# The rotated halves of retention's queries and keys: two VectorE products across partition halves in place of a TensorE product with a sign matrix

## The chip, the cores and the metric

One Trainium2 chip, one NeuronCore of it. The metric is the device time of the whole program in microseconds (us), the median of several executions. TensorE (PE), VectorE (DVE), ScalarE (ACT), GpSimd (POOL) and SyncE (SP, which here only issues DMA) each run a program of their own and meet only at semaphores.

## The reference

Two blocks of two layers each are run one after the other on 512 positions of width 1024, all in float32. The change lies in the first block. Each of its two layers has three branches (a gated MLP, a retention branch, a gated delta rule). What matters here is the retention branch, four heads of width 128:

```python
def rotary(x):
    ...
    x1, x2 = x[..., : hd // 2], x[..., hd // 2:]
    return jnp.concatenate([x1 * cos - x2 * sin, x2 * cos + x1 * sin], axis=-1)

def retention_branch(q, k, v, z, decay_logit, norm_g):
    q = rotary(q)
    k = rotary(k) * (RET_HD ** -0.5)
    ...                      # scores = q k^T times a decay mask, then times v, over all 512 positions
```

So each of the 8 tiles (4 heads of q, 4 of k) needs x * cos plus the tile with its two halves swapped, one of them negated, times sin.

## The kernel before

Activations are held feature-major: a tile is 128 features (partitions) by 512 positions. Weights come in granules of 512 KB that SP loads into four buffers `raw`; ACT rounds each to `wh` (`hi`, L1688), POOL computes the rest `wl = raw - wh` in two instructions of 128x512 (L2288), and PE multiplies with both parts of both operands, so one output tile is 8 x 3 matrix products of 128x512 (`feature_tile`, L827 to L829). A granule's buffer is reused four granules later; ACT rounds the next one right after it has copied the finished tile out of PSUM.

Granules 12 to 19 of each layer are the four query tiles and the four key tiles of retention. For each, in order of i = 0 to 7:

- PE runs `feature_tile(12 + i)`. After i = 0 it adds a few small products (`decay_sums`), after i = 1 the 16 products of `token_mix` for the gated MLP. From i = 1 on it then runs `rotate(i - 1)`, one float32 product of the sign matrix `rot` with tile i - 1, and after the last tile also `rotate(7)`. `rotate` writes one of PSUM banks 4 to 7 (bank 7 and 6 are called `pair` in the rows). It waits for ACT's copy of the tile, and for the bank to be free (`y_ready` for the first four, `rot_taken` for the others).
- ACT copies the finished tile to `qraw[i % 4]` (L1748; from i = 4 on it waits for `rot_taken` of tile i - 4), then rounds the granule g + 4.
- DVE first finishes `token_mix` (L2609, L2610), prepares two decay masks (`mask_arg`, L2617 to L2619), and then for each tile forms `rt2` = rotated x sin (L2626), `rt1` = qraw x cos (L2627) and their sum (L2630), into `rqT` for queries and into a part of `y` for keys.

Then PE runs `scores(0)` (L983, four products), and for each head `scores(h + 1)` and the products with the values (L994). DVE multiplies each score tile by its mask (`pb`, L2637) and frees its bank; `scores(1)` waits for the first `pb` of head 0. DVE executes in program order, so it comes to the first `pb` only when all eight tiles are rotated. Twelve more feature tiles (20 to 31) follow, with retention's normalisation and turns (`retention_turns`, L1004) between the first of them.

The DVE program has its own semaphore on which `step` and `inc` wait after each instruction. DVE_OWN counts such steps.

Of the kernel before, what the change touches and what calls it, by code (L numbers as in the profile page):

```python
# [18 lines left out]
ALU = mybir.AluOpType  # L19
# [3 lines left out]
P = 128  # L23
# [16 lines left out]
SUB = 1 << BASE  # L40
# [9 lines left out]

CON = {}
_at = 0
for _name, _n in (("ident", 128), ("ones", 128), ("rot", 128), ("cos", 512), ("sin", 512), ("dist", 896),
                  ("tri", 256), ("neg", 256), ("level", 2 * LEVELS * 128), ("own", 4), ("turn", 4)):
    CON[_name] = slice(_at, _at + _n)
    _at += _n
# [3 lines left out]
def constants():  # L60

    c = np.zeros((P, N_CON), np.float32)
    i = np.arange(P)
    c[:, CON["ident"]] = np.eye(P)
    c[:, CON["ones"]] = 1.0
    rot = np.zeros((P, P), np.float32)
    rot[i[:64] + 64, i[:64]] = -1.0
    rot[i[:64], i[:64] + 64] = 1.0
    c[:, CON["rot"]] = rot
    inv = (np.float32(10000.0) ** (-np.arange(0, P, 2, dtype=np.float32) / np.float32(P))).astype(np.float32)  # L70
    ang = (np.arange(T, dtype=np.float32)[None, :] * inv[:, None]).astype(np.float32)
    c[:, CON["cos"]] = np.tile(np.cos(ang), (2, 1))
    c[:, CON["sin"]] = np.tile(np.sin(ang), (2, 1))
    c[:, CON["dist"]] = np.arange(896)[None, :] - i[:, None] - 384
    before = (i[:, None] <= i[None, :]).astype(np.float32)
    c[:, CON["tri"]] = np.concatenate([before, before.T], 1)
    c[:, CON["neg"]] = (np.concatenate([before, before.T], 1) - 1.0) * np.float32(1e30)
    level = np.zeros((P, 2, LEVELS, P), np.float32)
    for s in range(LEVELS):
        b = SUB << s  # L80
        same = (i[:, None] // (2 * b)) == (i[None, :] // (2 * b))
        m = same & ((i[:, None] // b) % 2 == 0) & ((i[None, :] // b) % 2 == 1)
        level[:, 0, s] = m
        level[:, 1, s] = m.T
    c[:, CON["level"]] = level.reshape(P, -1)
    c[:, CON["own"]] = (i[:, None] // SUB) == np.arange(4)[None, :]
    forward = (i % SUB) < SUB // 2
    c[:, CON["turn"]] = np.stack([np.where(forward, 1.0, -1.0), forward, ~forward, 0.0 * i], 1)
    return c
# [39 lines left out]
def layer_signals(nc):  # L129
    per = dict(  # L130
        x_ready=8, sq_ready=8, sq_added=6, norm_sd=1, norm_rec=1, ht_ready=8, hh_ready=8, hl_ready=8,
        proj_taken=44, wab_hi=1, wab_lo=1, ab_rows=1, ab_done=3, beta_ready=1, log_args=2, log_done=2,
        g_ready=1, egc_ready=1, nbeg_ready=1, norm_spread=2, l2_spread=8,
        vhat_sd=4, vhat_ready=4, lnvar=4, mix_done=4, y_ready=8, y_gated=8,
        rot_done=8, rot_taken=8, rope_ready=8,
        arg_ready=4, mask_ready=4, score_done=16, p_ready=16, o_done=4, o_taken=4,
        gn_var=1, gn_sd=1, gn_ready=4, gn_turned=4,
        conv_ready=12, silu_ready=12, nsq_ready=8, l2_done=8, l2_sd=8, l2_rec=8, l2_ready=8,
        kt_done=4, ktok_ready=4, vt_done=4, vtok_ready=4,
        blocks_done=1, blocks_out=2, arg_small=1, exp_small=1, solved=2, gz_ready=4, gz_taken=4,  # L140
        rows_done=8, kq_done=4, ag_ready=8, e_ready=16, lt_ready=8, st_ready=8, ub_ready=8,
        last_ready=8, qg_ready=8, lm_ready=16, y0_ready=8, x0_ready=8,
        p1_done=16, p1_ready=16, a_done=16, inv_ready=24,
        rhs_ready=24, wt_done=8, wt_ready=8,
        vn_done=32, vn_ready=32, s_done=24, s_ready=24, out_done=32, go_sq=4, go_ss=8, go_sd=4, go_rec=4, yc_raw=4,
        z_mul=4,
        yh_ready=12, yl_ready=12, gate_taken=24, merged=24, mh_ready=8, ml_ready=8, xl_ready=8,
        dve_own=DVE_OWN, act_own=ACT_OWN,
    )
    return {k: Signal(nc, k, v) for k, v in per.items()}  # L150

DVE_OWN = 126 + 2 * (SUB - 1)
ACT_OWN = 3


# [299 lines left out]
def build(nc, stream, params, consts, consts2, gains, xin, memin, out, n_granules):  # L457
    cur = [16512]

    def sb(name, shape, dt=F32, at=None):  # L460
        size = -(-int(np.prod(shape[1:])) * 4 // 32) * 32
        if at is None:
            at = cur[0]
            cur[0] += size
        assert at + size <= 229344, name
        return nc.alloc_sbuf_tensor_at(name, shape, dt, offset=at)
# [35 lines left out]
    C = {k: con[:, v] for k, v in CON.items()}  # L502
# [5 lines left out]
    ident, ones = C["ident"], C["ones"]  # L508
# [20 lines left out]
    qraw = [sb(f"qraw{i}", [P, T]) for i in range(4)]  # L529
    mask = [sb(f"mask{i}", [P, 896]) for i in range(2)]  # L530
    mtmp = sb("mtmp", [P, 896])
    rt2 = sb("rt2", [P, T])
# [78 lines left out]
    spare = sb("spare", [P, 1])  # L611
# [3 lines left out]
    for i in range(2):  # L615
        def tiles_at(n, count, at, shape=(P, T), dt=F32):
            return [sb(f"{n}_{i}_{t}", list(shape), dt, at=at + t * int(np.prod(shape[1:])) * 4) for t in range(count)]
        b = BUF[i]
# [51 lines left out]
    bk = [b[:, :] for b in bank] + [pair[:, 0:T], pair[:, T:2 * T]]  # L670
# [66 lines left out]
    with block:  # L737
# [85 lines left out]
        def _(pe):  # L823
            mm = nc.tensor.matmul
# [23 lines left out]
            with pe.Fori(0, DEPTH) as L:  # L848
                G = L * G_LAYER

                def wait(sig, n):
                    pe.wait_ge(s[sig].sem, s[sig].at(L, n))

                def inc(ins, sig):
                    ins.then_inc(s[sig].sem, 1)
# [20 lines left out]
                def feature_tile(g):  # L876

                    weights(g)
                    taken(g)
                    w = g % SLOTS  # L880
                    for k in range(KD):
                        m = three(bk[g % 4], wh[w][:, k * P:(k + 1) * P], wl[w][:, k * P:(k + 1) * P],
                                  hh[:, k], hl[:, k], k == 0, k == KD - 1)
                    m.then_inc(granule_done, 1)
# [53 lines left out]
                def decay_sums():  # L938

                    wait("g_ready", 1)  # L940
                    wait("beta_ready", 1)
                    for d in range(2):
                        m = mm(bk[6][:, 64 + d * 16:80 + d * 16], tri[d], gdec[:, :, d, :], start=True, stop=True)
                    inc(m, "ab_done")
# [10 lines left out]

                def rotate(i):
                    wait("proj_taken", 13 + i)
                    if i < 4:  # L960
                        wait("y_ready", i + 1)
                    else:
                        wait("rot_taken", i - 3)
                    inc(mm(bk[4 + i % 4], C["rot"], qraw[i % 4][:, :], start=True, stop=True), "rot_done")

                for i in range(8):
                    feature_tile(12 + i)
                    if i == 0:
                        decay_sums()
                    if i == 1:  # L970
                        token_mix()
                    if i:
                        rotate(i - 1)
                rotate(7)

                def scores(h):
                    wait("rope_ready", 5 + h)
                    for b in range(NT):
                        if h:
                            wait("p_ready", 4 * h + b - 3)  # L980
                        else:
                            wait("rot_taken", 5 + b)
                        inc(mm(bk[4 + b], rkT[h][:, b * P:(b + 1) * P], rqT[h][:, :], start=True, stop=True),  # L983
                            "score_done")

                scores(0)
                for h in range(H):
# [3 lines left out]
                    for b in range(NT):  # L991
                        wait("p_ready", 4 * h + b + 1)
                        for c in range(NT):
                            m = mm(bk[h][:, c * P:(c + 1) * P], pb[h % 2][b][:, c * P:(c + 1) * P], rv[b][:, h * P:(h + 1) * P],  # L994
                                   start=(b == 0 and c == 0), stop=(b == NT - 1), skip_group_check=True)
# [68 lines left out]
                for h in range(H):  # L1064
# [62 lines left out]
                    for st in range(NT):  # L1127
                        for d in range(2):
                            c = st if d == 0 else NT - 1 - st
# [13 lines left out]
                        for d in range(2):  # L1143
                            c = st if d == 0 else NT - 1 - st
# [1366 lines left out]
        def _(dve):  # L2511
            V = nc.vector
# [27 lines left out]
            with dve.Fori(0, DEPTH) as L:  # L2540
                step = Steps(dve, s["dve_own"], L)

                def wait(sig, n):
                    dve.wait_ge(s[sig].sem, s[sig].at(L, n))
# [3 lines left out]
                def inc(ins, sig):  # L2548

                    ins.then_inc(s[sig].sem, 1)  # L2550
                    count[sig] += 1
                    wait(sig, count[sig])
# [69 lines left out]
                mask_arg(1)  # L2622

                for i in range(8):
                    wait("rot_done", i + 1)
                    step(V.tensor_tensor(rt2[:, :], bk[4 + i % 4], C["sin"], ALU.mult))  # L2626
                    inc(V.tensor_tensor(rt1[:, :], qraw[i % 4][:, :], C["cos"], ALU.mult), "rot_taken")  # L2627
                    wait("rot_taken", i + 1)
                    dst = rqT[i][:, :] if i < 4 else rkT[i - 4]
                    inc(V.tensor_tensor(dst, rt1[:, :], rt2[:, :], ALU.add), "rope_ready")  # L2630
# [116 lines left out]
                for h in range(H):  # L2747
# [37 lines left out]
                    for st in range(NT - 1):  # L2785
                        for d in range(2):
                            c = st if d == 0 else NT - 1 - st
# [15 lines left out]
                with dve.Fori(0, 3) as n:  # L2803
                    B = L * 3 + n
                    G = L * G_LAYER
                    wait("dve_own", DVE_OWN)
                    for q in range(2):
# [552 lines left out]
```

## Time and profile before

| | |
|---|---|
| median of 3 runs | 2737.86 us (2737.37 to 2738.4) |
| profiled execution, first to last instruction | 2738.6 us |
| TensorE busy | 2660.0 us, 97% |
| VectorE busy | 1084.0 us, 40% |
| ScalarE busy | 1139.7 us, 42% |
| GpSimd busy | 1384.8 us, 51% |

The profile gives one execution's span, no other time of it; that span is 0.7 us above the median of the runs. The first layer's tiles 12 to 19 and its scores lie at about 94 to 180 us, the second layer's 677.4 us later. Matrix products are pipelined, so a row of 0.39 us does not mean that the next one starts 0.39 us later.

### The profile page before, as it was taken

What the parts mean: (1) busy time and instruction counts of PE and PEld (TensorE: products, weight loads), DVE (VectorE), ACT (ScalarE), POOL (GpSimd) and SP (SyncE); (2) the same over time, 40 slices, a digit from 0 to 9 for tenths busy, and PEclk for the clock granted to TensorE, in tenths of its full rate; (3) what the DMA queues carried; (4) which work ended last, traced back from release to release, by engine and by line L of the source; (5) the groups of instructions that cost most, each with busy time, mean ns of one, the idle gap of its engine ahead of it and who ended that gap; (6) DMA issues with size and microseconds to landing.
All of it is one profiled execution on the core that took longest, in us unless ns stands there. A gap on an engine that the chain in (4) does not pass through costs nothing.

```text
span 2738.6 us, 37589 instructions
## 1 busy us (share of the span) xinstructions
PE 2660.0 (97%) x13032; PEld 2158.2 (79%) x13032; DVE 1084.0 (40%) x2191; ACT 1139.7 (42%) x1732; POOL 1384.8 (51%) x1056
## 2 busy tenths in 40 slices
PE   7999999999999999999999999999999989999999
PEld 6768898888876889888887647888887755888887
DVE  3576643113466664312366563211104375221100
ACT  5437444324542744432455643333315464333321
POOL 5424665556642466655674213556547502466553
PEclk9999999999999999999999999999999999999999
DMA  5212111233221211123332112232333301233322
GB/s 179 83 44 75 41 32 40 99 99 125 86 85 39 70 40 31 47 93 99 123 103 75 32 31 70 93 100 92 100 113 109 92 8 40 78 108 98 100 93 76
DMA packets 62351, 215.10 MB, mean 79 GB/s; under 512 B 7296, under 2 KB 10496, under 8 KB 61824
## 3 DMA queue, kind: packets, MB, share of 16 engines
q1 hardware_dynamic: 62208, 213.28, 24.3%
q8 instruction: 79, 1.29, 0.2%
q14 instruction: 64, 0.52, 0.1%
HBM read 211.16 MB, written 2.10 MB: 78 GB/s over the span
## 4 chain that ended last, share of the span: by engine, by line
PE 82%; DVE 9%; issue 4%; POOL 2%; ACT 1%; DMA 0%; POOLq 0%; DVEq 0%; SPq 0%; ACTq 0%
PE bank L827 21%; PE bank L829 21%; PE bank L828 21%; PE pair L827 2%; PE pair L829 2%; PE pair L828 2%; PE pair L1530 2%; PE bank L994 1%; PE bank L1489 1%; PE bank L1490 1%; PE bank L1512 1%; DVE pair L2712 1%; DVE prod L2711 1%; POOL EG L2366 1%; PE pair L1343 1%
## 5 line engine op out<-in xcount | busy, mean ns | idle before, releaser
L2288 POOL TENSOR_TENSOR wl<-raw,wh 128x512 fp32r<-128x512 f32 x768 | 1036.3, 1373 | 1175.5 <-ACT wh L1919 380.8
L827 PE MATMUL bank<-hh,wh 128*128 128x512 f32 x1536 | 607.4, 395 | 3.7 <-DVE y L2799 2.3
L829 PE MATMUL bank<-hh,wl 128*128 128x512 f32 x1536 | 599.0, 390 | 0.0
L828 PE MATMUL bank<-hl,wh 128*128 128x512 f32 x1536 | 598.9, 390 | 0.0
L827 PEld LDWEIGHTS bank<-hh,wh 128*128 128x128 f32 x1536 | 289.1, 188 | 66.5 <-issue 5.6
L828 PEld LDWEIGHTS bank<-hl,wh 128*128 128x128 f32 x1536 | 289.1, 188 | 61.7 <-issue 2.9
L829 PEld LDWEIGHTS bank<-hh,wl 128*128 128x128 f32 x1536 | 288.9, 188 | 60.9
L2239 ACT CAST wh<-raw 128x1024 fp32r<-128x1024 f32 x120 | 125.5, 1048 | 254.0 <-PE pair L829 140.2
L827 PE MATMUL bank<-wh,hh 128*128 128x512 f32 (+2 forms) x352 | 140.6, 399 | 13.8 <-POOL wl L2288 12.4
L1919 ACT CAST wh<-raw 128x1024 fp32r<-128x1024 f32 x84 | 86.9, 1048 | 128.0 <-PE bank L829 108.5
L829 PE MATMUL bank<-wh,hl 128*128 128x512 f32 (+2 forms) x352 | 135.1, 384 | 0.0
L828 PE MATMUL bank<-wl,hh 128*128 128x512 f32 (+2 forms) x352 | 135.0, 384 | 0.0
L2812 DVE TENSOR_TENSOR gs<-gs,bank 128x512 f32<-128x512 f32 x24 | 16.4, 684 | 286.3 <-PE bank L829 286.3
L1688 ACT CAST wh<-raw 128x1024 fp32r<-128x1024 f32 x104 | 108.9, 1049 | 42.9 <-DMA raw<-stream 18.8
L1872 ACT CAST wh<-raw 128x1024 fp32r<-128x1024 f32 x72 | 75.3, 1046 | 85.5 <-PE pair L829 43.8
L3186 DVE TENSOR_TENSOR at<-row,bank 128x512 f32<-128x512 f32 x44 | 30.3, 689 | 202.2 <-PE bank L829 199.4
L827 PE MATMUL bank<-ah,wh 128*128 (+1 forms) x264 | 102.7, 389 | 0.0
L828 PE MATMUL bank<-al,wh 128*128 (+1 forms) x264 | 102.7, 389 | 0.0
L829 PE MATMUL bank<-ah,wl 128*128 (+1 forms) x264 | 102.7, 389 | 0.0
L1888 ACT ACTIVATE gs<-bank 128x512 f32<-128x512 f32 x48 | 28.8, 599 | 166.6 <-PE bank L829 166.5
L3183 DVE TENSOR_TENSOR at<-row,bank 128x512 f32<-128x512 f32 x44 | 30.3, 688 | 162.7 <-PE bank L829 162.1
L827 PEld LDWEIGHTS bank<-wh,hh 128*128 128x128 f32 x352 | 67.7, 192 | 26.1 <-issue 14.6
(465 smaller groups left out, 5235.8 us busy)
## 6 DMA issues: line engine op xcount, KB each, us to landing
raw<-stream SPq DMA_DIRECT2D x384, 512.0 KB, 3.5
mraw<-memin SPq DMA_DIRECT2D x3, 1024.0 KB, 5.5
par<-params SPq DMA_DIRECT2D x2, 1124.5 KB, 9.3
out<-xT SPq DMA_DIRECT2D x8, 256.0 KB, 2.0
con<-consts SPq DMA_DIRECT2D x1, 1540.0 KB, 15.7
xT<-xin SPq DMA_DIRECT2D x1, 1536.0 KB, 8.6
xT<-xin SPq DMA_DIRECT2D x1, 512.0 KB, 3.8
con<-consts SPq DMA_DIRECT2D x1, 512.0 KB, 3.2
```

Of the source, the lines that this page charges most:

```text
L827: mm(o, ah, bh, start=start, stop=False)
L828: mm(o, ah, bl, start=False, stop=False)
L829: return mm(o, al, bh, start=False, stop=stop)
L1530: x = mm(bk[value_bank(i, phase, a)], vv, pts[a % 2][kb][:, :], start=(kb == 0), stop=(kb == nk - 1))
L1688: nc.scalar.copy(wh[g % SLOTS][:, :], raw[g % SLOTS][:, :]).then_inc(hi_ready, 1)
L1872: nc.scalar.copy(wh[g % SLOTS][:, :], raw[g % SLOTS][:, :]).then_inc(hi_ready, 1)
L1888: A(gs[e][:, :], bk[e], ACT.Sigmoid).then_inc(s["gate_taken"].sem, 1)
L1919: nc.scalar.copy(wh[g % SLOTS][:, :], raw[g % SLOTS][:, :]).then_inc(hi_ready, 1)
L2239: nc.scalar.copy(wh[slot][:, :], raw[slot][:, :]).then_inc(hi_ready, 1)
L2288: m = TT(wl[slot][:, c], raw[slot][:, c], wh[slot][:, c].bitcast(F32), ALU.subtract)
L3183: V.tensor_tensor(at_[j][:, :], row[:, :], bk[2 * j], ALU.mult).then_inc(t["f_gate"].sem, 1)
L3186: V.tensor_tensor(at_[j][:, :], row[:, :], bk[2 * j + 1], ALU.mult).then_inc(t["f_up"].sem, 1)
```

## The change

The sign matrix goes from the constants (its 128 columns stay as unused space, so that no other column moves). `rotate` and its eight calls go from PE, with the signal `rot_done`. On DVE each tile's `rt2` now comes from `qraw` in two products of 64 partitions by 512: output partitions 0 to 63 from input partitions 64 to 127, and the other way round, with a sine table whose upper 64 rows carry the minus sign. Between these two and the product with the cosine there is no wait, where the `step` after L2626 was one. DVE waits for ACT's copy (`proj_taken`) instead of PE's product. `scores(0)` no longer waits for `rot_taken`.

```diff
-for _name, _n in (("ident", 128), ("ones", 128), ("rot", 128), ...
+for _name, _n in (("ident", 128), ("ones", 128), ("spare", 128), ...
...
-    rot = np.zeros((P, P), np.float32)
-    rot[i[:64] + 64, i[:64]] = -1.0
-    rot[i[:64], i[:64] + 64] = 1.0
-    c[:, CON["rot"]] = rot
...
-    c[:, CON["sin"]] = np.tile(np.sin(ang), (2, 1))
+    c[:, CON["sin"]] = np.concatenate([np.sin(ang), -np.sin(ang)])
...
-DVE_OWN = 126 + 2 * (SUB - 1)
+DVE_OWN = 118 + 2 * (SUB - 1)
...
-                def rotate(i):
-                    wait("proj_taken", 13 + i)
-                    if i < 4:
-                        wait("y_ready", i + 1)
-                    else:
-                        wait("rot_taken", i - 3)
-                    inc(mm(bk[4 + i % 4], C["rot"], qraw[i % 4][:, :], start=True, stop=True), "rot_done")
-
                 for i in range(8):
                     feature_tile(12 + i)
                     if i == 0:
                         decay_sums()
                     if i == 1:
                         token_mix()
-                    if i:
-                        rotate(i - 1)
-                rotate(7)
 
                 def scores(h):
                     wait("rope_ready", 5 + h)
                     for b in range(NT):
                         if h:
                             wait("p_ready", 4 * h + b - 3)
-                        else:
-                            wait("rot_taken", 5 + b)
...
                 for i in range(8):
-                    wait("rot_done", i + 1)
-                    step(V.tensor_tensor(rt2[:, :], bk[4 + i % 4], C["sin"], ALU.mult))
+                    wait("proj_taken", 13 + i)
+                    for low in (0, P // 2):
+                        to, of = slice(low, low + P // 2), slice(P // 2 - low, P - low)
+                        V.tensor_tensor(rt2[to, :], qraw[i % 4][of, :], C["sin"][of, :], ALU.mult)
                     inc(V.tensor_tensor(rt1[:, :], qraw[i % 4][:, :], C["cos"], ALU.mult), "rot_taken")
```

## Rows read from the trace of the kernel before

**Rows 1.** The page: busy time, and the chain that ended last.

```profile
PE 2660.0 (97%) x13032; PEld 2158.2 (79%) x13032; DVE 1084.0 (40%) x2191; ACT 1139.7 (42%) x1732; POOL 1384.8 (51%) x1056
...
PE 82%; DVE 9%; issue 4%; POOL 2%; ACT 1%; DMA 0%; POOLq 0%; DVEq 0%; SPq 0%; ACTq 0%
```

**Rows 2.** Chain in order of time, first layer (start us, us, what).

```profile
116.75 0.86 PE bank L964 x2
...
155.14 0.70 DVE pb L2637
155.88 1.98 PE bank L983 x4
```

**Rows 3.** Timeline of DVE, first layer.

```profile
119.05 2.06 DVE L2619 TENSOR_TENSOR mask<-mask,mtmp 128x896 f32<-128x896 f32 x1
...
143.10 0.69 DVE L2626 TENSOR_TENSOR rt<-bank,con 128x512 f32<-128x512 f32 x1 [3.23 <-PE bank L964]
143.82 0.69 DVE L2627 TENSOR_TENSOR rt<-qraw,con 128x512 f32<-128x512 f32 x1
144.62 1.60 DVE L2630 TENSOR_TENSOR y<-rt,rt 128x512 f32<-128x512 f32 x1
...
152.57 0.69 DVE L2626 TENSOR_TENSOR rt<-pair,con 128x512 f32<-128x512 f32 x1
153.30 0.91 DVE L2627 TENSOR_TENSOR rt<-qraw,con 128x512 f32<-128x512 f32 x1
154.31 0.69 DVE L2630 TENSOR_TENSOR y<-rt,rt 128x512 f32<-128x512 f32 x1
```

**Rows 4.** Timeline of POOL, first layer.

```profile
102.39 2.54 POOL L2288 TENSOR_TENSOR wl<-raw,wh 128x512 fp32r<-128x512 f32 x2 [2.13 <-ACT wh L1688]
...
118.54 3.72 POOL L2288 TENSOR_TENSOR wl<-raw,wh 128x512 fp32r<-128x512 f32 x2 [7.40 <-ACT wh L1688]
...
143.93 3.44 POOL L2288 TENSOR_TENSOR wl<-raw,wh 128x512 fp32r<-128x512 f32 x2 [2.91 <-ACT wh L1688]
150.27 3.39 POOL L2288 TENSOR_TENSOR wl<-raw,wh 128x512 fp32r<-128x512 f32 x2 [2.90 <-ACT wh L1688]
```

**Rows 5.** Timeline of ACT, first layer.

```profile
148.52 0.60 ACT L1748 ACTIVATE qraw<-bank 128x512 f32<-128x512 f32 x1 [3.81 <-PE bank L829]
```

**Rows 6.** Timeline of PE: first rotation, scores of head 1, products with the values.

```profile
110.16 1.10 PE L964 MATMUL bank<-qraw,con 128*128 128x512 f32 x2 [0.18 <-DVE y L2610]
...
159.42 3.73 PE L994 MATMUL bank<-rv,pb 128*128 128x128 f32 x32
...
833.31 3.57 PE L983 MATMUL bank<-rqT,y 128*128 128x512 f32 x4 [0.49 <-DVE pb L2637]
...
838.54 3.73 PE L994 MATMUL bank<-rv,pb 128*128 128x128 f32 x32
```

**Rows 7.** Stretches (PE busy and granted clock, PEclk): both layers, the waits for DVE.

```profile
198.69:202.10 3.41, 1.92 (x14) 1.27 (x13) 3.05 (x5) 2.59 (x4) 0.96 (x1) 1.00 0.03 13
...
830.17:833.57 3.40, 1.51 (x4) 0.56 (x4) 3.01 (x5) 0.00 (x0) 0.92 (x1) 1.00 0.42 118
833.57:836.98 3.41, 3.41 (x5) 1.34 (x5) 3.02 (x5) 0.00 (x0) 0.00 (x0) 0.50 0.09 36
...
878.00:881.35 3.35, 1.87 (x15) 1.27 (x13) 2.99 (x5) 2.71 (x4) 1.08 (x1) 1.00 0.06 22
881.40:888.10 6.70, 6.70 (x20) 5.44 (x20) 4.32 (x5) 1.59 (x3) 1.55 (x2) 0.50 0.26 78
```

**Rows 8.** Timeline of PE at the kernel's start.

```profile
12.44 0.79 PE L827 MATMUL bank<-wh,hh 128*128 128x512 f32 x1 [12.44 <-POOL wl L2288]
...
17.73 0.42 PE L827 MATMUL bank<-wh,hh 128*128 128x512 f32 x1
```

**Rows 9.** Timeline of DVE between the layers: neighbours with no wait between them.

```profile
684.46 0.67 DVE L2821 TENSOR_TENSOR xT<-xT,bank 128x512 f32<-128x512 f32 x1
685.06 0.74 DVE L2526 SCALAR_TENSOR_TENSOR hl<-xT,par,hh 128x512 fp32r<-128x512 f32 x1
```

More of the change, by code:

```diff
@@ L52 @@
 _at = 0
-for _name, _n in (("ident", 128), ("ones", 128), ("rot", 128), ("cos", 512), ("sin", 512), ("dist", 896),
+for _name, _n in (("ident", 128), ("ones", 128), ("spare", 128), ("cos", 512), ("sin", 512), ("dist", 896),
                   ("tri", 256), ("neg", 256), ("level", 2 * LEVELS * 128), ("own", 4), ("turn", 4)):
@@ L134, in layer_signals @@
         vhat_sd=4, vhat_ready=4, lnvar=4, mix_done=4, y_ready=8, y_gated=8,
-        rot_done=8, rot_taken=8, rope_ready=8,
+        rot_taken=8, rope_ready=8,
         arg_ready=4, mask_ready=4, score_done=16, p_ready=16, o_done=4, o_taken=4,
```

## The prediction

> **What bounds the kernel now.** I read the page first: PE is busy 97% of the span and holds 82% of the chain that ended last, DVE 9% [rows 1]. That says where time usually goes, not what this change meets, so I read the chain of waits through the stage of the change next. There PE passes from feature tile to feature tile, and each rotation stands in its path with 0.86 us (two passes of a float32 product) [rows 2]. At the stage's end the chain leaves PE: the last rotations and the first `pb` are DVE's, 155.14, and PE's scores of head 1 follow at 155.88 [rows 2]. So two clocks matter: PE's through the eight tiles, DVE's at the end. The timelines of DVE, POOL and ACT show how close they are.
>
> **What the change takes from PE.** Eight products per layer. Up to the end of tile 19 six of them lie on its path: the first costs its 0.86 plus 0.18 of waiting for `y` [rows 6], 1.0; five more 0.86 each [rows 2]. Together 5.3 us: ACT's copy of tile 19 starts at 143.2 instead of 148.52 [rows 5]. The last two rotations go from behind it. If nothing else held the stage, the first `pb` could come one rotation after that copy: 143.8 plus 3.0 (below), some 146.8, which is 8.3 us earlier than 155.14, in each layer.
>
> **What it gives to DVE.** Before, a tile cost product from PSUM, product with cosine, sum: starts at 143.82 and 144.62 give 0.80 from the second to the third; 152.57 and 153.30 give 0.73 from first to second; the sum takes 0.69 plus 0.03 [rows 3]. That is 2.25 us. After, there is one product more. No row shows a 64-partition operation. The nearest rows are products of the same 512 columns at 0.69 [rows 3]; bounds are 0.35 if half the partitions cost half, and 1.38 if a crossing costs double. I take 0.69, since nothing in the rows ties time to anything but columns. For the spacing of neighbours with no wait between them the rows give 0.60 (684.46 to 685.06) [rows 9], with a wait 0.73; I take 0.73, the nearer row, since it is the same kind of product in the same place. So 2.98 us per tile, 23.8 for eight. With the shorter spacing for the two freed gaps the eight tiles would take 8 x 2 x 0.13, some 2 us, less. The Trainium skill, "VectorE: DVE Perf Modes", section "Two Vector instructions with no wait between them", speaks for this choice: an instruction whose input or output starts in another group of 32 partitions than the last one's is held until the earlier ones are finished. By it the sum stays, without it the 2 us go; no row here shows a held pair.
>
> **What it takes away: PSUM was outside POOL's way.** The sum at 144.62 takes 1.60 instead of 0.69, and the cosine product at 153.30 takes 0.91; both read two SBUF operands while POOL works on `wl` [rows 3, 4]. The PSUM product at 152.57 keeps its 0.69 in the midst of POOL's pair 150.27 to 153.66. And POOL's pair grows from 2.54 undisturbed to 3.44 [rows 4]. The ends fit a strict alternation: POOL's first operation starts when the cosine product ends at 144.51, holds some 1.0 us, the sum runs 145.53 to 146.22, POOL's second ends at 147.37. So one POOL operation costs a waiting DVE product up to 1.0 us. Before, DVE idled between tiles and met POOL mostly once per tile. After, all four operations of a tile read SBUF, and DVE hardly idles.
>
> **The schedule of DVE, first layer.** It comes free for the rotations at 119.05 + 2.06 = 121.1 [rows 3]. POOL's pair for the tile that ends before was asked for at 118.54 [rows 4]; it comes 1.0 earlier (the first rotation is gone), falls before the last two mask operations instead of between them, and both its parts now delay them: DVE is free at 122.1. POOL's pair comes 1.75 us after a copy (150.27 behind 148.52) [rows 4, 5] and pairs are 6.34 apart (143.93 to 150.27), 5.5 without the rotation between. So the five further pairs are asked for at 145.0 for tile 19 and at about 139.5, 134.0, 128.5 and 123.0 before it. Ten operations, each holding DVE 0.95 (gaps take the rest), are 9.5. 122.1 + 23.8 + 9.5 = 155.4 for the end of the last sum; before it was 154.31 + 0.69 = 155.0 [rows 3]. DVE never waits for a copy on the way: the last at 143.8 is there long before the eighth tile's turn at 152.4. So the first `pb` comes 0.4 us later than before, less 0.1 for the freed waits: I take 0.3 per layer, 0.6 in all. The 8.3 us saved on PE turn into PE's wait for the first `pb`. `scores(0)` is done by 148 (it needs only the fifth rotation, at about 144.5, then 3.4 us), and behind it on PE's queue everything waits until about 156.2: 8 us. From there on both kernels run alike.
>
> **The clock.** That wait is longer than any in the middle of this kernel. In the second layer PE is busy 1.51 of 3.40 us, then the granted clock is 0.50, the lower of the two levels (1.2 GHz), for 3.41 us, and 1.00 after [rows 7]. Its price can be read: the products with the values start at 159.42 and 838.54, 679.12 apart, where the layers lie 677.43 apart (155.88 to 833.31, the scores just before): 1.7 us [rows 2, 6]. At the start of the kernel, after idleness, PE stays at the lower level from 12.44 until 17.7, 5.3 us [rows 8], worth 2.6; the fall at 881.40 lasts 6.70, worth up to 3.3 [rows 7]. The scores behind the new wait are bound by PE, so the price is paid. First layer, where there was no fall: bounds 1.7 and 3.3, I take 2.4. Second layer, which paid 1.7: bounds 0 and 1.6 more, I take 0.8. Sum 3.2.
>
> **Sum.** Rotations on DVE +0.6, clock +3.2: +3.8. Against the profiled span of 2738.6 this is 2742.4; that span stands 0.7 above the median, so 2741.7 for the median. One thing more may move with it, and I put it in the range only: at 878.00 PE is busy 1.87 of 3.35 and the clock falls for 6.70 us, while in the first layer 1.92 of 3.41 at 198.69 lead to no fall (1.00 there) [rows 7]. So close a decision can turn over when the stage arrives 3 us later, in either layer: plus or minus 3.3.
>
> **Rivals.** A measurement of this kernel can tell about 0.2%, 5.5 us, from no change.
>
> (a) DVE becomes the bound and gives all of PE's time back, the clock adds a little: +3.8, likeliest, 0.55. Its own range is 0 to +10, 2738 to 2748.
>
> (b) DVE keeps up. For it speaks that DVE idles 3.23 us before the sixth tile (143.10) [rows 3]. If the half products cost 0.35 each, the same schedule ends near 149.5, 5.6 earlier per layer; PE's idleness is then some 2 us, a fall as dear as the one there was: -11 +2, about 2729. If POOL did not stop it at all, near 146.9, 8.2 earlier per layer: 2721. Against it: rows tie cost to columns, and the stops are plain. Chance 0.13, 2721 to 2732.
>
> (c) DVE is slower than I count, and ends on the other side: a product that crosses partition halves costs more than one that does not. Sixteen of them per layer, with DVE the bound: each 0.1 us more is 3.2 us over both layers. From 0.12 more on the time is over the bound; at 1.38 each it would be +22, 2764. For it: no row shows one. Against it: nothing does so either. Chance 0.15, typically 2745 to 2765.
>
> (d) The neighbours with no wait overlap as in [rows 9]: 2 us less per layer, the wait shorter, one fall instead of more: about 2737. Chance 0.17. That the change does not take the rotations off PE at all is no case: the calls are gone.
>
> **How the numbers follow.** Slower by over 0.2% (above 2743.3): from (a) 0.17, where the clock turns over or falls twice, and (c) 0.12: 0.29. Faster (below 2732.4): (b) 0.12 and 0.01 of (d): 0.13. Within: 0.58. The range leaves out most of (b) and the far half of (c): 2732 to 2749.
>
> **What would show it.** Tile 19's copy near 143.2; sixteen half products per layer at 0.69 where POOL is still and up to 1.7 where it is not; no idle time of DVE between 122 and 155; PE without work from 148 to 156 with DVE named as releaser; first `pb` at 155.4; the granted clock at 0.50 behind it in both layers. A first `pb` before 152 would make the prediction wrong, and show that POOL's stops or the half products were counted too dear; one after 157 the reverse.

## The result, and the profile after

The kernel after takes 2746.78 us (median of 12 runs, 2744.95 to 2748.7), the kernel before 2738.86 (12 runs of the same sessions, 2736.18 to 2742.34). The ratio is 1.0026, 95% interval 1.0018 to 1.0035: 7.9 us slower by the medians. The likeliest case of the forecast said 3.8 slower, 2741.7; the range, 2732 to 2749, holds the time, which lies just past the 0.2% that the prediction called "slower" (it gave that a chance of 0.29; the interval begins at 0.18%). The profiled execution after has a span of 2744.2, against 2738.6 before. In every run on record the span is 1.8 us shorter than the run's time, so the execution profiled before stands for some 2740.4 us, 1.5 above its median, and the one after (2745.97) lies 0.8 below its own: the two profiles differ by 5.6 us, the medians by 7.9.

The page of the kernel after: busy time, then the chain that ended last, by engine ([rows 1] are before). PE is busy 7.9 us less, yet the span is longer: PE's idle time grew from 78.6 to 92.1 us, and of the work taken away (some 14 us, below) nearly half came back as a slower clock.

```profile
PE 2652.1 (97%) x13000; PEld 2156.0 (79%) x13000; DVE 1103.9 (40%) x2207; ACT 1140.0 (42%) x1732; POOL 1383.2 (50%) x1056
...
PE 80%; DVE 11%; issue 4%; POOL 2%; ACT 1%; DMA 0%; DVEq 0%; POOLq 0%; SPq 0%; ACTq 0%
```

The timeline of DVE after, first layer, against [rows 3]. Each tile is four operations now: two half products (L2611), the cosine product (L2612) and the sum (L2615).

```profile
120.90 1.09 DVE L2602 TENSOR_TENSOR mask<-mask,mtmp 128x896 f32<-128x896 f32 x1
122.11 2.40 DVE L2611 TENSOR_TENSOR rt<-qraw,con 64x512 f32<-64x512 f32 x2
124.53 1.69 DVE L2612 TENSOR_TENSOR rt<-qraw,con 128x512 f32<-128x512 f32 x1
126.31 0.69 DVE L2615 TENSOR_TENSOR rqT<-rt,rt 128x512 f32<-128x512 f32 x1
127.13 1.39 DVE L2611 TENSOR_TENSOR rt<-qraw,con 64x512 f32<-64x512 f32 x2
128.53 1.69 DVE L2612 TENSOR_TENSOR rt<-qraw,con 128x512 f32<-128x512 f32 x1
130.32 1.59 DVE L2615 TENSOR_TENSOR rqT<-rt,rt 128x512 f32<-128x512 f32 x1
...
152.73 1.39 DVE L2611 TENSOR_TENSOR rt<-qraw,con 64x512 f32<-64x512 f32 x2
154.13 0.69 DVE L2612 TENSOR_TENSOR rt<-qraw,con 128x512 f32<-128x512 f32 x1
154.92 0.69 DVE L2615 TENSOR_TENSOR y<-rt,rt 128x512 f32<-128x512 f32 x1
155.75 1.50 DVE L2622 SCALAR_TENSOR_TENSOR pb<-bank,mask 128x512 f32<-128x512 f32 x2
```

Two half products take 1.39 together, as much as two whole ones. Four of the eight operations from 122.11 to 131.9 take 0.9 to 1.0 too long; that is POOL, whose pairs of the same stretch were

```profile
117.23 3.16 POOL L2271 TENSOR_TENSOR wl<-raw,wh 128x512 fp32r<-128x512 f32 x2 [6.06 <-ACT wh L1671]
122.67 2.99 POOL L2271 TENSOR_TENSOR wl<-raw,wh 128x512 fp32r<-128x512 f32 x2 [2.29 <-ACT wh L1671]
128.24 3.12 POOL L2271 TENSOR_TENSOR wl<-raw,wh 128x512 fp32r<-128x512 f32 x2 [2.58 <-ACT wh L1671]
```

No row of this stage has a bracket: DVE waits for nobody from 122 to 155.

ACT's copy of tile 19 after, against [rows 5]:

```profile
142.67 0.60 ACT L1731 ACTIVATE qraw<-bank 128x512 f32<-128x512 f32 x1 [2.90 <-PE bank L825]
```

It comes 5.85 us earlier, and nothing is gained by it. The timeline of PE after shows where the time goes, against [rows 6]:

```profile
144.79 1.98 PE L966 MATMUL bank<-rqT,y 128*128 128x512 f32 x4 [2.16 <-DVE y L2615]
146.61 1.88 PE L966 MATMUL pair<-rqT,y 128*128 128x512 f32 x4
156.50 3.78 PE L966 MATMUL bank<-rqT,y 128*128 128x512 f32 x4 [8.00 <-DVE pb L2622]
160.07 2.39 PE L966 MATMUL pair<-rqT,y 128*128 128x512 f32 x4
162.30 3.73 PE L977 MATMUL bank<-rv,pb 128*128 128x128 f32 x32
...
838.38 3.78 PE L966 MATMUL bank<-rqT,y 128*128 128x512 f32 x4 [6.31 <-DVE pb L2622]
841.96 2.78 PE L966 MATMUL pair<-rqT,y 128*128 128x512 f32 x4
844.57 3.73 PE L977 MATMUL bank<-rv,pb 128*128 128x128 f32 x32
```

PE waits 2.16 us for the fifth rotation and 8.00 for the first `pb`; in the second layer 2.1 and 6.31. The four products behind the wait take 3.78 instead of 1.98. The stretches of the kernel after (last columns: granted clock, DMA share, GB/s) say why, against [rows 7]:

```profile
150.85:161.09 10.24, 4.59 (x6) 2.02 (x7) 9.19 (x14) 0.00 (x0) 0.00 (x0) 0.50 0.01 2
...
202.06:205.47 3.41, 1.92 (x16) 1.60 (x16) 3.09 (x4) 2.81 (x4) 1.48 (x2) 1.00 0.02 7
205.47:208.88 3.41, 3.41 (x11) 2.73 (x11) 3.23 (x4) 1.55 (x2) 1.21 (x1) 0.50 0.29 50
...
836.93:843.75 6.82, 5.37 (x7) 2.27 (x8) 6.02 (x9) 0.24 (x1) 0.00 (x0) 0.50 0.01 2
888.13:891.50 3.37, 3.37 (x9) 2.60 (x9) 3.21 (x4) 1.52 (x2) 0.84 (x1) 0.50 0.35 95
```

The products with the values start at 162.30 against 159.42 before, +2.9: 0.6 of it is the later first `pb` (155.75 against 155.14), the rest PE's 4.59 us of work at the lower level. A new fall at 205 follows; the second layer's first query tile is copied at 782.40 against 777.93, +4.5, and at the end of its stage the products with the values stand at 844.57 against 838.54, +6.0.

### The profile page after: what moved, and what is told of

It is laid out like the page before. It is cut to its first block, busy times and chain, and to the rows that moved or that the text cites. A ratio compares the mean times of both kernels' runs of the same rounds, so it can differ in the third digit from the quotient of the medians.

```text
span 2744.2 us, 37499 instructions
## 1 busy us (share of the span) xinstructions
PE 2652.1 (97%) x13000; PEld 2156.0 (79%) x13000; DVE 1103.9 (40%) x2207; ACT 1140.0 (42%) x1732; POOL 1383.2 (50%) x1056
## 3 DMA queue, kind: packets, MB, share of 16 engines
q8 instruction: 79, 1.29, 0.2%
## 4 chain that ended last, share of the span: by engine, by line
PE 80%; DVE 11%; issue 4%; POOL 2%; ACT 1%; DMA 0%; DVEq 0%; POOLq 0%; SPq 0%; ACTq 0%
PE bank L823 20%; PE bank L825 20%; PE bank L824 20%; PE pair L823 2%; PE pair L825 2%; PE pair L824 2%; PE pair L1513 2%; DVE rt L2611 1%; PE bank L977 1%; PE bank L1472 1%; PE bank L1473 1%; PE bank L1495 1%; DVE pair L2697 1%; DVE prod L2696 1%; POOL EG L2349 1%
## 5 line engine op out<-in xcount | busy, mean ns | idle before, releaser
L823 PE MATMUL bank<-wh,hh 128*128 128x512 f32 (+2 forms) x352 | 141.0, 400 | 13.8 <-POOL wl L2271 12.4
L823 PEld LDWEIGHTS bank<-wh,hh 128*128 128x128 f32 x352 | 68.0, 193 | 26.2 <-issue 14.6
```

The source lines that it names most:

```text
L823: mm(o, ah, bh, start=start, stop=False)
```

## Experiments

Each ran beside the kernel before, on the same chip as that. Where the clock falls for 6.83 instead of 3.41 us at the kernel's start, everything in that trace starts 1.6 to 1.8 us later; where a `pb` is compared below, this is taken off ("net"). Times are medians; in brackets the 95% interval of the ratio.

**1. Fill PE's new wait** (`e1_filler`)

```diff
                 scores(0)
+                wait("proj_taken", 17)
+                for _ in range(8):
+                    mm(bk[0], ident, rqT[0][:, :], start=True, stop=True)
```

> The changed kernel with eight float32 products of 128x512 (0.86 us each, 6.9 us) put on PE behind the scores of head 0, into bank 0, whose result is overwritten. They fill most of the 8.0 us in which PE waits for the first pb. Theory (the wait costs twice: once by itself, once by the lower clock behind it): first pb stays at 155.75 us, but the granted clock stays 1.00 behind it, the first product with the values starts near 160.1 instead of 162.30, and the second layer gains about 1.7; the program comes to about 2743, 3 to 4 us under the changed kernel. Rival (the fall of the clock is not due to the wait, or costs nothing because DVE sets the pace there): no change within 1 us.

2739.65 us, 1.0001 [0.9991, 1.001]: the slowdown is gone, with work added and none taken away. The timeline of PE and a stretch of that kernel:

```profile
149.78 7.03 PE L972 MATMUL bank<-rqT,con 128*128 128x512 f32 x16
156.64 1.88 PE L966 MATMUL bank<-rqT,y 128*128 128x512 f32 x4
```

```profile
150.00:157.00 7.00, 7.00 (x17) 3.04 (x16) 6.36 (x10) 0.00 (x0) 0.00 (x0) 1.00 0.04 14
```

The first `pb` came at 155.56, 0.2 sooner than after; what is different is the clock behind it (1.88 us for four products, not 3.78), and the products with the values start at 160.08, as expected. In this execution the clock fell earlier instead, under the scores of head 0 (four products in 3.62 us from 144.60). By the medians this is worth 7.1 us, more than the 3 to 4 expected; the section below returns to that.

**2. Take POOL out of DVE's way, after and before** (`e2_nolow`, `e5_before_nolow`): the low parts of six weight granules are computed for 8 columns only.

```diff
                 for g in range(5, 36):
-                    lo(g)
+                    if 18 <= g < 24:
+                        pool.wait_ge(hi_ready, G + g + 1)
+                        w = g % SLOTS
+                        TT(wl[w][:, 0:8], raw[w][:, 0:8], wh[w][:, 0:8].bitcast(F32), ALU.subtract).then_inc(lo_ready, 1)
+                    else:
+                        lo(g)
```

> The changed kernel; POOL leaves out all but 8 columns of the low parts wl of granules 18 to 23 of both layers, so those weights' low parts are stale and the output is not the reference's. Theory (POOL's operations stop DVE's two-SBUF-operand products and so make DVE the bound): every product on DVE takes 0.69, eight tiles take some 24 us from about 120, the last tile waits for ACT's copy (143.3), first pb at 147 to 148 instead of 155.75, time about 8 us less per layer plus the clock: 2728 to 2732. Rival (the sixteen half products by themselves are too much for DVE): first pb not before 153, gain under 6 us in all.

> The kernel before, with POOL's low parts of granules 18 to 23 cut to 8 columns as in the run without low parts (weights stale there, so the output is not the reference's). Theory (POOL's stops cost the kernel before little, since DVE read PSUM in one operation of three and idled between tiles; they became dear with the change): first pb 1 to 1.5 us earlier than 155.14, 1 to 2 us less per layer, 2734 to 2737. Rival (POOL's work weighs as much there, and the gain of 20 us of the run without low parts is not the change's): 2725 or less.

After with the cut: 2719.04, 0.9924 [0.991, 0.9937], 27.7 us below the kernel after. Before with the cut: 2735.84, 0.9986 [0.9977, 0.9996], 3.6 us. The same POOL work costs the one kernel almost eight times what it costs the other. DVE in the first:

```profile
120.26 1.39 DVE L2616 TENSOR_TENSOR rt<-qraw,con 64x512 f32<-64x512 f32 x2
121.66 0.69 DVE L2617 TENSOR_TENSOR rt<-qraw,con 128x512 f32<-128x512 f32 x1
122.46 0.69 DVE L2620 TENSOR_TENSOR rqT<-rt,rt 128x512 f32<-128x512 f32 x1
123.27 1.39 DVE L2616 TENSOR_TENSOR rt<-qraw,con 64x512 f32<-64x512 f32 x2
...
143.27 1.39 DVE L2616 TENSOR_TENSOR rt<-qraw,con 64x512 f32<-64x512 f32 x2 [2.03 <-ACT qraw L1731]
...
146.29 1.51 DVE L2627 SCALAR_TENSOR_TENSOR pb<-bank,mask 128x512 f32<-128x512 f32 x2
```

An undisturbed tile takes 3.01 us (120.26 to 123.27), DVE keeps up with ACT and waits for the last copy, and the first `pb` comes 9.5 us sooner. That is 1 to 2 us more than was expected, and the time lies 9 us below the expected 2728; the clock has part in it, for this kernel's mean is 0.9976, the highest of all.

**3. One whole product in place of two halves; the halves without the crossing** (`e3_one`, `e6_uncrossed`)

```diff
-                    for low in (0, P // 2):
-                        to, of = slice(low, low + P // 2), slice(P // 2 - low, P - low)
-                        V.tensor_tensor(rt2[to, :], qraw[i % 4][of, :], C["sin"][of, :], ALU.mult)
+                    V.tensor_tensor(rt2[:, :], qraw[i % 4][:, :], C["sin"], ALU.mult)
```

```diff
                     for low in (0, P // 2):
-                        to, of = slice(low, low + P // 2), slice(P // 2 - low, P - low)
+                        to = of = slice(low, low + P // 2)
```

> The changed kernel with one product of 128x512 (qraw times sine, halves not crossed, so the output is not the reference's) in place of the two half products. Theory (a half product costs as much as a whole one, and DVE sets the end of the stage): a tile is 0.70 us shorter, first pb near 150 instead of 155.75, 5 to 6 us less per layer, the program 2732 to 2736. Rival (half products cost half): first pb within 0.5 us of 155.75 and no gain.

> The changed kernel with both half products reading the same partitions that they write (halves not swapped, so the output is not the reference's); everything else as it is. Theory (64 partitions cost as much as 128 and crossing costs nothing; neighbours are held because they begin in different partitions, swapped or not): half products 0.69 each, two in 1.39, the next one 0.70 to 0.71 behind the second; first pb within 0.3 of 155.75; time within 0.1% of the changed kernel. Rival (crossing halves costs time): two in 1.3 or less and first pb at least 1 us earlier.

Without the crossing: 2746.45, 1.0024 [1.0012, 1.0036], first `pb` at 155.69; nothing changed, so the crossing costs nothing. With one product: 2737.65, 0.9992 [0.9983, 1.0001]. Its `pb` came net some 6.5 us sooner (150.95 in a trace that starts late), where eight operations of 0.69 are 5.5; the total fell by 9.1 to a time above the expected 2732 to 2736. One reason lies outside the stage: in this kernel PE waits for DVE and POOL in other places too, 5.6 us more than before in all (its idle time is 88.2 against 78.6, of which the two stages are 4.0). The largest of these waits is one that the kernel before does not have:

```profile
PE pair L823 <- DVE inv L2697: 3.3, 2, 1.7
```

Two neighbours with no wait between them, in `e3_one` and then in `e6_uncrossed`:

```profile
127.84 0.69 DVE L2609 TENSOR_TENSOR rt<-qraw,con 128x512 f32<-128x512 f32 x1
128.45 0.68 DVE L2610 TENSOR_TENSOR rt<-qraw,con 128x512 f32<-128x512 f32 x1
```

```profile
132.00 1.39 DVE L2611 TENSOR_TENSOR rt<-qraw,con 64x512 f32<-64x512 f32 x2
133.40 0.69 DVE L2612 TENSOR_TENSOR rt<-qraw,con 128x512 f32<-128x512 f32 x1
```

Both starting at partition 0, they are 0.61 apart and overlap as in [rows 9]; with starts at partitions 0 and 64 in turn, 0.70 (1.39 for two, the next 1.40 behind the first). The freed waits paid only where the start does not change; with a change they save 0.03 us each (0.70 against 0.73).

**4. Bring the first `pb` forward in DVE's order** (`e4_inter`): six rotations, `pb` of head 0, then a rotation ahead of heads 1 and 2 each.

```diff
-                for i in range(8):
+                def rope(i):
...
+                for i in range(6):
+                    rope(i)
                 for h in range(H):
+                    if h in (1, 2):
+                        rope(5 + h)
...
-                    if h + 2 < H:
+                    if h in (1, 2):
                         wait("p_ready", 4 * h + 4)
-                        mask_arg(h + 2)
+                        mask_arg(h + 1)
```

> The changed kernel with DVE's order changed: it rotates six tiles, multiplies head 0's scores by the mask, rotates tile 6, head 1's scores, mask of head 2, rotates tile 7, and so on. Theory (PE waits for the first pb only because DVE's order puts it behind all eight rotations): first pb near 150.0, scores of head 1 near 150.7 instead of 156.5, no fall of the clock before them, rotations 6 and 7 under PE's products; 5 to 6 us less per layer plus 2 of clock, the program about 2732, under both kernels. Rival (DVE's work is the bound wherever it stands): PE waits later instead, for the rotation of tile 7 or for head 2's pb, and the program gains under 4 us on the changed kernel.

2730.87, 0.9966 [0.9952, 0.9979]. PE:

```profile
152.19 3.13 PE L966 MATMUL bank<-rqT,y 128*128 128x512 f32 x4 [1.98 <-DVE pb L2627]
```

The wait fell from 8.00 to 1.98 (first `pb` at 151.45, net 149.7, as expected), and the kernel is faster than before with every operation of the kernel after still in it: the order alone is worth 15.9 us against the kernel after. One thing did not come as expected: the clock still fell behind the wait, as the 3.13 us for four products show.

**5. The key tiles' products read the PSUM bank instead of the SBUF copy** (`e7_psum`, on top of 4). PE now waits for these reads before it overwrites the bank (first line).

```diff
+                    wait("rot_taken", 5 + h)
...
+                    src = qraw[i][:, :] if i < 4 else bk[i - 4]
...
-                        V.tensor_tensor(rt2[to, :], qraw[i % 4][of, :], C["sin"][of, :], ALU.mult)
-                    inc(V.tensor_tensor(rt1[:, :], qraw[i % 4][:, :], C["cos"], ALU.mult), "rot_taken")
+                        V.tensor_tensor(rt2[to, :], src[of, :], C["sin"][of, :], ALU.mult)
+                    inc(V.tensor_tensor(rt1[:, :], src, C["cos"], ALU.mult), "rot_taken")
```

> The interleaved kernel (pb of head 0 behind six rotations), and for the four key tiles the sine and cosine products read the tile from PE's PSUM bank instead of ACT's copy; PE waits for these reads before it writes the bank again. Theory (a product with one operand in PSUM is not stopped by POOL): the products of tiles 16 and 17 take 0.69 in the midst of POOL's pairs, only the sums are stopped, first pb 2 to 3 us earlier than in the interleaved kernel (151.45 there, with a start 1.75 later), PE's wait for it under 1.5 us; 2722 to 2727. Rival (PSUM operand or not, POOL stops them): within 2 us of the interleaved kernel.

2725.5, 0.9949 [0.9932, 0.9965], within what was expected; first `pb` at 149.29, 2.2 sooner than in 4. DVE, and POOL in the same stretch:

```profile
145.67 1.39 DVE L2613 TENSOR_TENSOR rt<-bank,con 64x512 f32<-64x512 f32 x2
147.07 0.69 DVE L2614 TENSOR_TENSOR rt<-bank,con 128x512 f32<-128x512 f32 x1
```

```profile
146.11 2.50 POOL L2272 TENSOR_TENSOR wl<-raw,wh 128x512 fp32r<-128x512 f32 x2 [2.43 <-ACT wh L1672]
```

The products run at full pace in the midst of POOL's pair, and the pair takes 2.50, not the 3.12 of the same pair after (3.11 in 4). The sum behind them, whose operands are both in SBUF, still took 1.29.

**6. The change for the first three tiles only** (`e8_three`, made from the kernel before, with the signed sine table and a sign matrix to suit it)

```diff
-                    if i:
+                    if i > 3:
                         rotate(i - 1)
...
-                    wait("rot_done", i + 1)
-                    step(V.tensor_tensor(rt2[:, :], bk[4 + i % 4], C["sin"], ALU.mult))
+                    if i < 3:
+                        wait("proj_taken", 13 + i)
+                        for low in (0, P // 2):
+                            to, of = slice(low, low + P // 2), slice(P // 2 - low, P - low)
+                            V.tensor_tensor(rt2[to, :], qraw[i % 4][of, :], C["sin"][of, :], ALU.mult)
+                    else:
+                        wait("rot_done", i - 2)
+                        step(V.tensor_tensor(rt2[:, :], bk[4 + i % 4], C["sin"], ALU.mult))
```

> The kernel before with the change for the first three tiles only (DVE's half products; the other five rotated by PE with the sign matrix as before). Theory (PE's time is saved as long as DVE catches up before the last tile): 2.7 us off PE's path, DVE late until about tile 17 and then in step, tile 19's copy near 145.8, first pb near 152.4 against 155.14, no longer wait of PE than before; 5 to 6 us less over both layers, 2733 or so. Rival (each half product and POOL's stops delay DVE to the end): first pb at 154.5 or later and no gain.

2733.29, 0.998 [0.997, 0.999]: 6.2 less than before, where six rotations of 0.86 are 5.2. The first `pb` stands at 153.42, net 151.7, and PE waits no longer than before (1.33 and 0.49). Where DVE has slack, the change does what it is for.

**7. The first two masks into DVE's idle time** (`e9_masks`; `e10_all` with 4 and 5; `e11_before_masks` alone). DVE idles 8.5 us ahead of the decay sums, and the masks stood behind them, in front of the rotations.

```diff
...
+                mask_arg(0)
+                mask_arg(1)
+
                 wait("ab_done", 3)
                 wait("egc_ready", 1)
...
-                mask_arg(0)
-                mask_arg(1)
```

> The changed kernel with the first two decay masks (six DVE operations, 5.3 us and more with POOL's stops) moved ahead of DVE's wait for the decay sums, where DVE idles 8.5 us. Theory (the change fails on DVE's late start, 122.1, and its full schedule from there): rotations begin near 114.7, DVE is in step with PE from about the sixth tile, first pb near 148.3 instead of 155.75, PE's wait near 2 to 3 us instead of 8, 7 us less per layer plus clock: 2726 to 2731. Rival (POOL's stops alone keep DVE behind, wherever it starts): first pb at 152 or later, 2738 or more.

> The kernel with pb of head 0 behind six rotations and the key tiles read from PSUM, with the masks moved as in the run before it. Theory: PE no longer waits more than 1 us for the first pb, scores of head 1 near 146.5 to 147.5, 3 us earlier per layer than with the masks in their place: 2718 to 2722. Rival (what is left is PE's own work or a wait for the masks of heads 2 and 3): 2724 to 2727, as without the move.

> The kernel before with the same move of the two masks. Theory (there the end of the stage hangs on PE's last rotations, DVE had caught up by the fourth tile anyway): first pb within 0.3 of 155.14, time within 0.1% of the kernel before. Rival (the move is worth its 5 us everywhere): 2730 or less.

Moved in the kernel before: 2739.22, 0.9999 [0.9989, 1.0009], nothing. In the kernel after: 2732.15, 0.9979 [0.9967, 0.9991], 1 us above what was expected: the rotations begin 7.35 us sooner (114.76) but meet one more pair of POOL's, so the first `pb` comes at 150.43, not 148.3, and PE waits 5.1 us, not 2 to 3. With all three: 2717.17, 0.9916 [0.9899, 0.9932], the fastest kernel of all, 22 us below before and 29.6 below after. PE no longer waits for the first `pb` at all, and DVE waits for PE again:

```profile
145.33 0.69 DVE L2629 SCALAR_TENSOR_TENSOR pb<-bank,mask 128x512 f32<-128x512 f32 x1 [3.87 <-PE bank L966]
```

## Why the prediction was right, and where its sizes were off

**PE's saving.** Predicted: copy of tile 19 at 143.2. Measured 142.67. Right in kind, 0.5 short in size: ACT's copies stand 6.35 us apart before (142.17 to 148.52) and 5.44 after (137.23 to 142.67), so a rotation took 0.91 of PE's path and not 0.86, and the first one 1.31 with its wait. It cost the forecast nothing, since DVE sets the end.

**DVE becomes the bound.** Predicted: free for the rotations at 122.1, eight tiles of 2.98, ten POOL operations of 0.95, last sum ending 155.4. Measured: 122.11 and 155.61. From 122.11 to the `pb` at 155.75 are 33.64 us; eight undisturbed tiles of 3.01 (experiment 2) are 24.1, which leaves 9.5 for POOL, the term predicted (the ten stops, added up from the rows, are 9.5 too). So the first `pb` was 0.61 late per layer, not 0.3: a tile takes 3.01, not 2.98 (from a sum to the next tile 0.81, not 0.72), and the 0.1 taken off for freed waits was not there.

**POOL's stops.** DVE's slack is used up by both, the extra product and POOL's stops. Without the stops the kernel is 20.2 us faster than before, with its extra product still in it (experiment 2); without the extra product the first `pb` comes 6.5 us sooner, with the stops still in it (experiment 3). The stops are the larger part, 9.5 us against 5.5. The Trainium skill, "SBUF — State Buffer", section "Who interferes with whom", states that a DVE instruction with two SBUF inputs contends with a GpSimd instruction that reads SBUF, and that one with at most one SBUF input does not, outside the 2-port modes. The products of 1.69 beside POOL's pairs and of 0.69 in experiment 5 agree. One SBUF operand is no safeguard for every operation here: the mask operations of L2600 and L2601 read one SBUF tensor only (896 columns in 0.69 us undisturbed, as long as 512 columns of a product), and two of them took 1.60 beside the pair that starts at 117.23, which would fit the exception, though no row names the mode. That the prediction had, when it put DVE's start at 122.1.

**Half products, crossing, neighbours.** 0.69 for 64 partitions as for 128, and no price for the crossing: rivals (b) and (c) fall (experiment 3). Of (b) the second leg is confirmed by experiment 2: it said 2721 for a kernel that POOL does not stop. (In (c) the step from which the bound of 5.5 us is passed should be 0.05, not 0.12: 5.5 less 3.8, shared among 32 products.) Rival (d) falls too: the neighbours do not overlap, 0.70 apart, and 0.61 once the start partition stays. The Trainium skill, "VectorE: DVE Perf Modes", section "Two Vector instructions with no wait between them", states that an instruction is held when its input or output starts in another group of 32 partitions than the one before; these rows agree with both sides of it.

**PE's wait.** Predicted 8 us from 148 to 156.2; measured 8.00 to 156.50. The 2.16 for the fifth rotation ahead of it was not named; it costs nothing of its own, since `pb` is late anyway.

**The clock: right inside the stages, too small for the whole (the term that was mis-sized).** Predicted 2.4 and 0.8, in all 3.2, for the two stages, and nothing outside them but plus or minus 3.3. Rows of ACT and PE that stand in both traces show how late the kernel after is, and where it becomes so:

| up to | late by, us | what came in the stretch |
|---|---|---|
| first products with the values | 2.9 | first `pb` 0.6, clock 2.3 |
| ACT's row at 213.57 (209.14 before) | 4.4 | the new fall at 205, 3.41 us |
| first products with the values, second layer | 6.0 | first `pb` 0.6, clock 0.9 |
| ACT's row at 1399.74 (1395.78 before) | 4.0 | the fall of [rows 7] at 881 lasts 3.37 instead of 6.70 |
| ACT's row at 1421.15 (1415.46 before) | 5.7 | a fall of 3.41 at 1403.6 before lasts 6.83 at 1407 |
| end | 5.6 | a fall of 3.41 at 2103 before lasts 6.81 at 2106, at no cost |

Inside the stages the clock cost 2.3 + 0.9 = 3.2, the term as predicted (another fall, at 826.69, lies ahead of the second wait and only shortens it, from 8.0 to 6.31). Outside them the falls did not stay as they were: one came, one shrank, two grew, 1.2 us in sum. With 1.2 for the first `pb` that makes the 5.6 of the profiles. That the outside falls nearly cancel in this pair of executions is luck, and no term of the prediction: in the medians, whose difference is 7.9, some 3.5 us are left for them.

How much of it is clock can be read from the runs themselves, because a kernel's mean granted clock is not the same in each of its runs. Of the 63 runs of the kernel before that stood beside the experiments, 13 had 0.998 with a mean span of 2735.2, 25 had 0.997 with 2736.9, 16 had 0.996 with 2739.5, 5 had 0.994 with 2742.5; the line through all 63 falls by 2.0 us for each 0.001. The kernel after had 0.991 to 0.993 in all its 12 runs (mean 0.9919), before 0.9965 to 0.9966 on average. The table gives for each kernel PE's work and waits against the kernel before, their sum, and the sum with 2.0 us added for each 0.001 that its mean clock lies below 0.9965 (taken off above it):

| kernel | PE's work, us | PE's waits, us | mean clock | work + waits | with clock | measured |
|---|---|---|---|---|---|---|
| after | -13.8 | +14.4 | 0.9919 | +0.6 | +9.8 | +7.9 |
| e6_uncrossed | -13.8 | +14.4 | 0.9919 | +0.6 | +9.8 | +7.0 |
| e1_filler | 0 | 0 | 0.9966 | 0 | -0.2 | +0.5 |
| e3_one | -13.8 | +4.0 | 0.9945 | -9.8 | -5.8 | -1.6 |
| e9_masks | -13.8 | +6.0 | 0.9943 | -7.8 | -3.4 | -7.1 |
| e4_inter | -13.8 | +3.4 | 0.9956 | -10.4 | -8.6 | -8.3 |
| e7_psum | -13.8 | +1.8 | 0.9970 | -12.0 | -13.0 | -14.0 |
| e10_all | -13.8 | -4.2 | 0.9968 | -18.0 | -18.6 | -22.0 |
| e2_nolow | -13.8 | -2.2 | 0.9976 | -16.0 | -18.2 | -20.2 |
| e8_three | -5.2 | -0.6 | 0.9966 | -5.8 | -6.0 | -6.2 |
| e5_before_nolow | 0 | -2.4 | 0.9972 | -2.4 | -3.8 | -3.6 |
| e11_before_masks | 0 | 0 | 0.9965 | 0 | 0 | 0.0 |

Work is 16 rotations of 0.86 (six in `e8_three`); `e1_filler` puts as many products back. Waits are PE's in both stages: 8.0 + 2.2 + 6.3 + 2.1 after, less 4.2 before (1.4, 0.5 and 0.2 in each layer). Measured is the median less that of the kernel before beside it. Work and waits alone leave `after` at +0.6, that is, at no change; the clock makes it slower. So the prediction had the right mechanism, and 3.2 for a term that the filler (7.1) and the mean clock (9.2) put at 7 to 9 in the runs. It took its price from the fall directly behind the wait, and the later falls only as plus or minus 3.3.

The same reading fits why `e1_filler` gained 7.1 by the medians and 3.0 by the profiles: its profiled run had 0.994, one of three such among eleven (2742.8 us of span on average), while the other eight had 0.997 to 0.999 (2734 to 2738).

**Left open.** The balance misses single kernels by up to 4.2 us. Two of its simplifications can be put right from the traces: with 0.91 for a rotation the work is 14.6 and not 13.8, and `e3_one` has the 5.6 us of further waits shown above. With both, `e3_one` comes out at -1.0 (measured -1.6), `e7_psum` at -13.8 (-14.0) and `after` at +9.0 (+7.9); the largest misses left are 2.9 in `e9_masks` and 2.6 in `e10_all`. A part of a fall that lies inside a wait costs nothing and is counted here all the same (of the 10.24 us at 0.50 in the kernel after PE was busy 4.59), so the clock's share is rather too large than too small for the kernels with long waits. The link of time and mean clock over the runs is a correlation; what shows the cause is `e1_filler`, in which only the wait was filled. Why a wait in the stage should bring falls tens or hundreds of microseconds later was not tried apart from that, and stays open: in the profiled execution of `e1_filler`, with its 0.994, falls of 6.8 us at 881.8, 1404 and 2103.8 were still there. And the falls outside the stages are not the change's alone: `e11_before_masks`, which keeps all rotations on PE, shows one of 3.4 us at 204.9 and one of 6.8 at 2102.7.

## What to carry to other kernels

Taking work from the engine that bounds a kernel pays only up to the point where the helper finishes last: read how much slack the helper has in that stage, less every stop by a neighbour. Here three tiles of eight paid 6 us and all eight lost 8. An operand's memory is part of an operation's price: a product with one operand in PSUM was outside POOL's way, and the same product with both in SBUF took up to 1.7 us instead of 0.69. When the helper is the bound, look at its order before giving the work back (first what the first consumer needs; what nobody waits for into its idle time), and compare the mean granted clock of the runs before explaining a few microseconds.

## What was not expected of the hardware

One and the same kernel has runs that differ by 8 us, and what differs with them on record is the mean granted clock. `e9_masks` ran four times with a mean granted clock of 0.992 to 0.993 (2737.75 to 2738.38 us) and six times with 0.994 to 0.996 (2729.68 to 2733.6), and no run between. A median of such a kernel says which group had more runs. The kernel after ran always in the low group, its filled twin mostly in a high one.

A pair of POOL's also gains when it is left alone: 3.12 us after, 2.50 in `e7_psum` for the same granule (the pair that starts at 144.42 and, in a trace 1.7 us later, at 146.11).
